# An inverse root as one power on GpSimd, in a two-layer hybrid decoder step

## The reference, cut to what matters

```
h = rms_norm(x, norm_g);  z = h @ w_in            # one wide projection
y_ret, y_gdn, y_sc, y_pool = four branches of z
proj = ys @ w_branch; gates = sigmoid(z[merge])   # per branch 512 -> 2048
merged = sum(gates * proj);  x = x + merged @ w_out
```

```
def _rms_norm(x, g):
    y = xf * lax.rsqrt(jnp.mean(xf * xf, axis=-1, keepdims=True) + EPS)
    return (y * g).astype(x.dtype)
o = _rms_norm(o, gdn_norm_g)
y_gdn = o.reshape(Bn, T, BW) * silu(gdn_gate)
```

## Time and profile before

| | us |
|---|---|
| median of 3 runs | 2033.35 (2031.99 to 2034.66) |
| profiled execution, its own time | 2032.6 |
| its span, first to last instruction | 2031.0 |
| TensorE (PE) busy | 1975.2 (97%) |
| VectorE (DVE) busy | 1346.3 (66%) |
| ScalarE (ACT) busy | 1112.8 (55%) |
| GpSimd (POOL) busy | 188.6 (9%) |
| HBM traffic | 170 GB/s mean |

### The profile page before, as it was taken

One profiled execution on the slowest core, in us unless ns is written; L12 is line 12 of the kernel. 1 busy time (PEld: TensorE's weight loads), 2 busy tenths in 40 slices (PEclk: granted clock), 3 DMA queues, 4 the chain that ended last, 5 costly groups with the idle time before them and its releaser, 6 DMA issues.

```text
span 2031.0 us, 50340 instructions
## 1 busy us (share of the span) xinstructions
PE 1975.2 (97%) x16166; PEld 1959.1 (96%) x16166; DVE 1346.3 (66%) x2608; ACT 1112.8 (55%) x2045; POOL 188.6 (9%) x345
## 2 busy tenths in 40 slices
PE   6999999999999999999999999999999999999996
PEld 6999999999999999999999999999999999999996
DVE  7887566755656566666678766676565656566666
ACT  5556556645455555555555655665454646455554
POOL 2111100110101010000011210001010100000000
PEclk9999999999999999999999999999999999999998
DMA  6655555555554545665666555655555555566564
GB/s 206 190 174 174 167 181 165 186 162 157 161 168 148 172 147 173 184 181 178 179 178 183 172 172 164 191 164 177 166 156 162 163 161 156 160 176 181 175 184 160
DMA packets 183252, 348.13 MB, mean 171 GB/s; under 512 B 20592, under 2 KB 20720, under 8 KB 182992
## 3 DMA queue, kind: packets, MB, share of 16 engines
q1 hardware_dynamic: 177552, 326.45, 53.4%
q0 software_dynamic: 5568, 19.80, 3.0%
HBM read 333.61 MB, written 12.56 MB: 170 GB/s over the span
## 4 chain that ended last, share of the span: by engine, by line
PE 90%; DVE 3%; issue 2%; ACT 2%; DMA 1%; DVEq 0%; SPq 0%; ACTq 0%
PE acc L1301 27%; PE acc L1302 27%; PE acc L1303 27%; DMA raw<-w_stream 1%; PE side L1514 1%; PE side L1488 1%; DVE wlo L829 1%; PE side L1512 1%; PE side L1495 1%; PE side L1402 1%; ACT whi L540 1%; PE side L1358 1%; DVE share L1082 0%; DVE wide L852 0%; PE side L1505 0%
## 5 line engine op out<-in xcount | busy, mean ns | idle before, releaser
L829 DVE TENSOR_TENSOR wlo<-raw,whi 128x512 fp32r<-128x512 f32 x1219 | 830.3, 696 | 477.2 <-ACT whi L540 469.8
L540 ACT ACTIVATE whi<-raw 128x512 fp32r<-128x512 f32 x1219 | 750.9, 628 | 630.0 <-PE acc L1303 542.6
L1301 PE MATMUL acc<-act_hi,whi 128*128 128x264 f32 x3328 | 971.8, 292 | 38.6 <-issue 17.0
L1303 PE MATMUL acc<-act_hi,wlo 128*128 128x264 f32 x3328 | 946.7, 284 | 0.0
L1302 PE MATMUL acc<-act_lo,whi 128*128 128x264 f32 x3328 | 946.4, 284 | 0.0
L1301 PEld LDWEIGHTS acc<-act_hi,whi 128*128 128x128 f32 x3328 | 631.2, 190 | 46.5 <-issue 33.8
L1302 PEld LDWEIGHTS acc<-act_lo,whi 128*128 128x128 f32 x3328 | 632.2, 190 | 1.0
L1303 PEld LDWEIGHTS acc<-act_hi,wlo 128*128 128x128 f32 x3328 | 628.4, 189 | 0.0
L1301 PE MATMUL acc<-y_hi,whi 128*128 128x264 f32 x1536 | 439.9, 286 | 0.0
L1302 PE MATMUL acc<-y_lo,whi 128*128 128x264 f32 x1536 | 435.4, 283 | 0.0
L1303 PE MATMUL acc<-y_hi,wlo 128*128 128x264 f32 x1536 | 434.9, 283 | 0.0
(11 more groups left out here) (267 smaller groups left out, 1406.1 us busy)
## 6 DMA issues: line engine op xcount, KB each, us to landing
raw<-w_stream SPq DMA_DIRECT2D x1220, 256.0 KB, 2.8
state<-ret_in POOLq DMA_DIRECT2D x8, 512.0 KB, 5.0
s_ret<-state POOLq DMA_DIRECT2D x8, 512.0 KB, 4.7
state<-gdn_in POOLq DMA_DIRECT2D x8, 512.0 KB, 6.0
s_gdn<-state POOLq DMA_DIRECT2D x8, 512.0 KB, 4.7
x<-x_in SPq DMA_DIRECT2D x4, 528.0 KB, 6.5
y_out<-wide SPq DMA_DIRECT2D x4, 396.0 KB, 2.8
con<-consts SPq DMA_DIRECT2D x1, 1582.0 KB, 11.6
```

The lines of the kernel that those rows point to most:

```text
L540: sc.activation(whi[:, s, :], raw[:, s, :], ACT.Copy).then_inc(hi_ready, 1)
L829: ve.tensor_tensor(wlo[:, s, :], raw[:, s, :], whi[:, s, :].bitcast(F32), ALU.subtract).then_inc(lo_ready, 1)
L1301: mm(acc[bank][:, 0:N], w_h, hi[:, k0 + k, :], start=first and k == 0, stop=False)
L1303: op = mm(acc[bank][:, 0:N], w_l, hi[:, k0 + k, :], start=False, stop=last and k == UK - 1)
```

## The change

The reciprocal on VectorE, the square root on ScalarE and the semaphore between them are gone. GpSimd, after issuing the write of the prompt state, waits for the mean square and computes `orc = oms ^ -0.5`, with the exponent read from a one-column tile `half` stretched over the columns. The multiplication by norm weight and gate stands after step 56 of VectorE's list instead of after step 54, the rounding to `y_hi` after step 57 of ScalarE's instead of 55, and `y_lo` after step 58 of VectorE's instead of 55. GpSimd's wait for its own prompt-state write, and with it the release of `pstate` and the next head's state load, now stands behind the power.

```
+        half = sb("half", [1])
+            gp.memset(half[:, :], -0.5).then_inc(half_set, 1)
             gp.memset(ab[:, :], 0.0).then_inc(zeros_set, 1)
+            pool.wait_ge(half_set, 1)
...
                     pool.dma_start(p_gdn[l, 0, h], pstate[:, 1, :]).then_inc(pstate_written, 16)
+                    pool.wait_ge(go_step, it * 4 + 1)
+                    gp.tensor_tensor(orc[:, :], oms[:, :], half[:, 0:1].to_broadcast([P, N]), ALU.pow).then_inc(go_step, 1)
                     pool.wait_ge(pstate_written, (it + l * BT) * 16 + 16 * BT + 16)
                     pool.sem_inc(pstate_free, 1)
...
                     sc.activation(osq[:, :], osb[:, :], ACT.Square).then_inc(go_copied, 1)
-                    units(49, 54)
-                    act.wait_ge(go_step, it * 4 + 2)
-                    sc.activation(oms[:, :], orc[:, :], ACT.Sqrt).then_inc(gors_ready, 1)
-                    units(54, 56)
+                    units(49, 58)
                     act.wait_ge(go_step, it * 4 + 4)
                     sc.activation(y_hi[:, bass.ds(h + YT[GDN], 1), :], y32[:, 0, :], ACT.Copy).then_inc(gyhi, 1)
-                    units(56, 60)
+                    units(58, 60)
...
                     ve.tensor_scalar(oms[:, :], side[2][:, 0:N], 1.0 / P, EPS, ALU.mult, ALU.add).then_inc(go_step, 1)
-                    dve.wait_ge(go_step, it * 4 + 1)
-                    ve.reciprocal(orc[:, :], oms[:, :]).then_inc(go_step, 1)
-                    units(52, 55)
-                    dve.wait_ge(gors_ready, it + 1)
-                    ve.scalar_tensor_tensor(out=orc[:, :], in0=osb[:, :], scalar=col(par, Q_GNG + l), in1=oms[:, :],
+                    units(52, 57)
+                    dve.wait_ge(go_step, it * 4 + 2)
+                    ve.scalar_tensor_tensor(out=orc[:, :], in0=osb[:, :], scalar=col(par, Q_GNG + l), in1=orc[:, :],
                                             op0=ALU.mult, op1=ALU.mult).then_inc(go_step, 1)
...
-                    units(55, 56)
+                    units(57, 59)
                     dve.wait_ge(gyhi, it + 1)
                     ve.tensor_tensor(y_lo[:, bass.ds(h + YT[GDN], 1), :], y32[:, 0, :],
                                      y_hi[:, bass.ds(h + YT[GDN], 1), :].bitcast(F32), ALU.subtract).then_inc(y_ready[GDN], 1)
-                    units(56, 60)
+                    units(59, 60)
```

More of the change, by code:

```diff
@@ L281, in trunk @@
         sum_cleared = sem("sum_cleared")
+        half_set = sem("half_set")
         sq_ready, norm_mm, ms_ready, rms_ready, rstd_ready = [sem(n) for n in
@@ L309, in trunk @@
             "gem_ready", "gR_ready", "gT_mm", "gT_ready", "gX_mm", "gX_ready", "gD_mm", "gTR_ready")]
-        gsol_mm, gvn_ready, gst_mm, gst_ready, gks_mm, grhs_ready, gqd_ready, go_mm, go_copied, gss_mm, go_step, \
-            gors_ready = [sem(n) for n in ("gsol_mm", "gvn_ready", "gst_mm", "gst_ready", "gks_mm", "grhs_ready",
-            "gqd_ready", "go_mm", "go_copied", "gss_mm", "go_step", "gors_ready")]
+        gsol_mm, gvn_ready, gst_mm, gst_ready, gks_mm, grhs_ready, gqd_ready, go_mm, go_copied, gss_mm, go_step = \
+            [sem(n) for n in ("gsol_mm", "gvn_ready", "gst_mm", "gst_ready", "gks_mm", "grhs_ready",
+            "gqd_ready", "go_mm", "go_copied", "gss_mm", "go_step")]
         gdl_mm, gdecayed, gstate_new, gos_mm, gos_copied = [sem(n) for n in
```

## The result

| | before | after |
|---|---|---|
| median of 4 runs each, in turn on one chip, us | 2034.01 (2031.99 to 2035.32) | 2288.76 (2288.15 to 2289.26) |
| ratio, 95% interval | | 1.1249 [1.1234, 1.1264] |
| profiled execution, its own time / span, us | 2032.6 / 2031.0 | 2289.2 / 2287.6 |
| mean granted clock | 0.993 | 0.938 |

The change costs 12.5%. The forecast was 2050 with a range up to 2088: the sign was right, the size was missed by 239 us. The page of after says where to look: GpSimd's busy time is up by 336 us with 9 instructions more, and TensorE's share is down from 97% to 87%. The last line is the chain that ended last, to be held against the earlier trace rows.

What follows compares the result with a forecast made beforehand. TensorE was taken as the bound. Stalls of 1.65 us, 8 times (13.2 us), and 3.4 us of clock on the profiled 2032.6 gave 2049.2, hence a forecast of 2050 us, range 2030.5 to 2088.

Steps and rivals of the forecast that it cites:

- TensorE is the bound; what VectorE and ScalarE save is worth nothing.: At the head's end TensorE waits for neither engine, so removing reciprocal, root and table load was costed at 0.
- The moved product costs 0.: Gated product 2 to 3 units later in VectorE's and ScalarE's lists: cost 0 if the power ends before VectorE arrives.
- My second rival: The turn's end was late because of VectorE: up to 2 us gained in each of 6 turns, 2021 to 2028, chance 0.04.
- The power takes 5.3 us, at most 12.4.: Duration of one 264-column power on GpSimd, estimated from ratios: 5.3 us, bounds 0.62 and 12.4 us.
- 2085: Upper end, in us, of the forecast's own range, 2037 to 2085, stated for a power of 4 to 8.5 us.
- X: The duration of one power on GpSimd, taken as 5.3 us.
- The power holds VectorE; TensorE stops from X = 3.65 on.: VectorE's first `wlo` after the mean square ends 0.55 us behind the power; TensorE stalls X - 3.65 per head, 1.65 us.
- the prediction's first rival: Power short, or holding VectorE only in pieces, so TensorE never stops: 2033, within 2030.5 to 2036, chance 0.30.
- A wait for the root decides from about 9.5 us on.: If the power does not hold VectorE, only waiting for its result counts, from a power of about 9.5 us.
- The stops at the turn's end stay at 2.5.: TensorE's stops at the loop's branch were to remain about 2.5 us in the profile after.
- Clock, +3.4.: The new stalls bring about 2 more falls of the granted clock, costing 3.4 us.
- The state load in front of the code fetch: Later state load meets the branch's code fetch; turn-end stops grow from 2.5 to 3.3 us, 2041, chance 0.06.

Runs made afterwards that it cites:

- x5: Kernel before with reciprocal and root replaced by a GpSimd product, gated output at its old places, inverse root left out: 2033.22 us, ratio 0.9991.
- x6: Kernel before, reciprocal and square root kept, with the gated output 2 units later on VectorE and ScalarE: 2030.47 us, ratio 0.9976.
- x12: Kernel before, reciprocal and square root kept, with the gated output 3 units later and `y_lo` at the turn's very end: 2033.11 us, ratio 0.9991.
- x7: Changed kernel with the power over 48 of the columns only, root of the others left out: 2041.62 us, ratio 1.0033 to before.
- x1: Kernel before with eight extra GpSimd powers and products per layer in its idle stretch, outputs unused: 2038.63 us, before 2034.83 on the same chip.
- x3: Changed kernel with the power over 132 of the 264 columns only, root of the rest left out: 2119.27 us.
- x2: Changed kernel with a 264-column GpSimd product in place of the power, inverse root left out: 2028.43 us, ratio 0.9963 to before.
- x10: Kernel before, reciprocal and square root kept, with a 264-column GpSimd power beside it, output unused: 2141.56 us, before 2035.79.
- x4: Changed kernel, power kept, with the gated output at the old places, 2 units earlier on VectorE and ScalarE: 2323.43 us.

## Why the prediction was wrong

**TensorE is the bound; what VectorE and ScalarE save is worth nothing.** Right within 0.2% (x5: 0.9991 [0.9981, 1.0001]).

**The moved product costs 0.** Its cover was named rightly (the power must end before VectorE gets there) and was gone. Without the power the place is not neutral but better by 0.24% in x6, though not told from nothing a unit later (x12). I had read the stop at the turn's end as the loop's alone. Its length is; its start hangs on VectorE's `wlo` of the last unit, and that stood in the earlier trace rows side by side: 488.02 and 488.2. My second rival was thus right that VectorE took part, and wrong by its size: it gave up to 2 us a turn. The start moved by 0.4 us, and 0.3 of stop went in x6, nothing in x5 and x12.

**The power takes 5.3 us, at most 12.4.** This is the step that failed, the mis-sized term: it took 42.47. The lower bound (0.62) was a measured product; the upper one was 20 passes of that product, a number of passes that no row showed. Measured, it is 68. The honest upper end, with no row of any power, was open, and the range should have reached into the region where the root itself is late. Within the sum, 2085 belongs to X = 9; with X = 8.5 it gives 8 x 4.85 = 39 us of stops and 8.5 of clock, 2081.

**The power holds VectorE; TensorE stops from X = 3.65 on.** Wrong as a mechanism, and the second step that failed: but for at most 0.4 us at its start, the power lets `wlo` through. The earlier trace rows show the hold only for a plain product; the prediction's first rival said that the rows went no further. So the forecast's mechanism would not have come true with the X of 5.3 either: x7, with 8.05 us, for which the formula gives a stop of 4.4, has none before the turn's end. Had X been 42.47 and the hold real, the stop would have been 42.47 - 3.65 = 38.8 a head, 310 us; measured were 32.67. The Trainium skill's page SBUF — State Buffer, section "Who interferes with whom", makes the shared ports an exclusive lock, for which a VectorE instruction with two SBUF inputs contends with a GpSimd instruction that reads SBUF. The trace of x1 contradicts this for a power (32 `wlo` at 679 to 695 ns beside one) and agrees for the 1024-column product (0.55 us behind its end). The measurement decides. For the power's price, the Trainium skill's page GPSIMD Engine Reference, section 3.1, would have given an estimated 0.6 us at its rate for elementwise work; the trace has 42.47.

**A wait for the root decides from about 9.5 us on.** Right, though it stood in a rival and without its working: 9.80 in after and x3. Nothing in the forecast carried it on to an X of 42. With the measured X this sentence gives 8 x (42.47 - 9.5) = 264 us before the turn's ends and the clock, against 261.4.

**The stops at the turn's end stay at 2.5.** Wrong in after, where they vanish inside the longer stops (-15 us). **Clock, +3.4.** The sign was right; with 8 long stops TensorE's busy time grew by 9.6.

**The state load in front of the code fetch** I took at 0 and gave 0.06 as a rival, with stops of 3.3 us and 2041. x7 is that case, though with a power of 8.05 us and not a short one: 3.26 us and 2041.6. x2 shows that a short root on GpSimd avoids it (load at 479.64). The 2.5 us of branching that I put between the power and the load were not there: x7 issues the load as the power ends, at 486.44. So with my X the load would have been issued at 483.5, and no run has one between 8 and 1.5 us ahead of the branch.

**Left open.** Why VectorE is spared, whether the power reads its columns at its start and then computes, as the short holds suggest, or reads with pauses, is not seen. Also open are most of x6's gain, what sets the length of a branch without a state load, and why the load hurts most about 1 us ahead of it. A root with more time than a whole turn was not tried.

## What to carry to other kernels

Before an operation is moved to an engine on which no row shows it, measure it alone at its real width: one probe gave 0.16 us a column here, and that decided the case. Then ask what is queued behind it on its own engine, because x10 lost 106 us with nobody waiting for its result. And at the end of a loop's turn, keep large loads off the branch (0.84% here); to let the last thing that the branching engine needs come first started the branch 0.4 us earlier, and paid in x2 and x6 but not in x5 and x12.

## What the runs showed of the hardware that I had not expected

- A power on GpSimd (128 partitions, fp32, -0.5 stretched) takes 0.37 us + 0.161 us a column: 0.88 us for 3 columns, 8.04 for 48, 10.97 for 66, 21.44 for 132, 42.47 to 42.80 for 264. Of the 0.37 us no more is known than that it is left over. A product of 264 columns takes 0.63.
- GpSimd holds VectorE's two-operand `wlo` while it runs a plain 1024-column product (2.88 us instead of 0.69), and the `y_lo` beside the next such product (2.12 instead of 0.43). A power delayed only a `wlo` that began in its first 0.4 us, by 0.1 to 0.4 us; 32 others beside one took 0.68 to 0.70.
- A taken branch at the end of this loop held TensorE's sequencer 3.6 us in the mean where hardly any weights moved beside it, 3.9 to 4.4 with the stream of weights, and 4.4 to 5.25 with a 512 KB load of GpSimd's queue besides, longest when that was issued some 1.1 us ahead. Matmuls already queued covered at most 2.22 us of it; in x4, where they ran at the lower clock, 3.2 to 4.0.
- After a stop of 32.7 us the granted clock was at its lower level, 0.50 of 2.4 GHz, in the windows just after matmuls resumed, and back at 1.00 some 4 us later. The first 140 matmuls after such a stop took, at the six turn ends inside the loop, 1.4 to 2.1 us more than after a stop with no fall (17.08 us).
